# Differential attention: 1/rms of the output as a power on GpSimd in place of ScalarE's root and VectorE's reciprocal

## What is computed

```python
def rms_norm(x, g):
    x32 = x.astype(F32)
    y = x32 * lax.rsqrt(jnp.mean(x32 * x32, axis=-1, keepdims=True) + EPS)
    return (y * g.astype(F32)).astype(x.dtype)

def diff_attention_mixer(u_lat, u_ctx, w_in, w_out, qn_g, kn_g, lam_vecs, subln_g, ...):
    q, k, v, z = split(u @ w_in)            # per token, 16 heads
    q, k = rms_norm(q, qn_g), rms_norm(k, kn_g)     # over 64 features each, two halves per head
    # rotary on the latent tokens, then per head: softmax(q1 k1) - lam * softmax(q2 k2), times v
    def finish(o, z, n):
        o = rms_norm(o, subln_g) * (1.0 - lam_init)
        return (o.reshape(bsz, n, D_INNER) * jax.nn.silu(z)) @ w_out
```

## Time and profile before

| | us |
|---|---|
| median of 3 runs (lowest to highest) | 4143.25 (4135.88 to 4145.75) |
| the profiled execution's own time | 4144.13 |
| its span (first to last instruction) | 4142.5 |
| TensorE busy | 3833.1 (93%) |
| VectorE busy | 2058.4 (50%) |
| ScalarE busy | 1136.8 (27%) |
| GpSimd busy | 142.6 (3%) |

### The profile page before, as it was taken

The page is one execution under the profiler, slowest core; times in us unless marked ns, Lnnn a source line. Parts: engine busy times, 40 slices in busy tenths (PEclk is TensorE's granted clock), DMA queues, the critical chain, the costliest instruction groups (busy, mean ns, idle before and its releaser), DMA issues. The chain is left out here.

```text
span 4142.5 us, 44540 instructions
## 1 busy us (share of the span) xinstructions
PE 3833.1 (93%) x16250; PEld 2479.6 (60%) x16250; DVE 2058.4 (50%) x3726; ACT 1136.8 (27%) x2079; POOL 142.6 (3%) x227
## 2 busy tenths in 40 slices
PE   6998999998889999999999999999697999999989
PEld 2445688874445888866565656565354555555554
DVE  3743453533553635446666666666303555555540
ACT  1112100011331000103343444434100444444430
POOL 6500000000000000000000000000000000000000
PEclk8998899987998999889999999999899999999999
DMA  7521323321013332421010111111011121111111
GB/s 151 138 71 46 102 76 97 82 77 48 22 46 88 90 91 72 107 77 36 26 32 29 30 30 30 30 30 31 15 51 46 48 56 56 56 56 56 56 41 53
DMA packets 456432, 246.26 MB, mean 59 GB/s; under 512 B 44256, under 2 KB 448352, under 8 KB 456320
## 3 DMA queue, kind: packets, MB, share of 16 engines
q1 hardware_dynamic: 420384, 216.15, 18.8%
q0 software_dynamic: 14144, 28.36, 2.6%
q10 hardware_dynamic: 21792, 0.22, 0.4%
HBM read 229.83 MB, written 14.80 MB: 59 GB/s over the span
## 5 line engine op out<-in xcount | busy, mean ns | idle before, releaser
L1152 PE MATMUL bank<-hT,ring 128*128 128x512 f32 (+1 forms) x1664 | 634.0, 531 | 23.4 <-DVE hT L1527 19.8
L1628 PE MATMUL bank<-hT,ring 128*128 128x512 f32 (+1 forms) x1536 | 521.1, 491 | 21.0 <-DVE big L1880 16.3
L1152 PEld LDWEIGHTS bank<-hT,ring 128*128 128x128 f32 x1664 | 310.8, 191 | 300.8 <-issue 269.5
L1628 PEld LDWEIGHTS bank<-hT,ring 128*128 128x128 f32 x1536 | 287.4, 190 | 250.3 <-issue 212.5
L326 PE MATMUL bank<-big,ring 128*128 128x512 f32 (+1 forms) x1024 | 391.9, 546 | 12.1 <-DVE big L1892 8.4
L326 PEld LDWEIGHTS bank<-big,ring 128*128 128x128 f32 x1024 | 196.7, 192 | 206.0 <-issue 185.5
L1057 ACT ACTIVATE arena<-bank 128x512 f32<-128x512 f32 (+2 forms) x224 | 118.3, 528 | 461.7 <-PE bank L1050 461.6
L456 PE MATMUL bank<-big,arena 128*128 128x256 f32 x1024 | 228.8, 379 | 0.0
L456 PEld LDWEIGHTS bank<-big,arena 128*128 128x128 f32 x1024 | 194.6, 190 | 26.5
L1025 DVE CUSTOM_DVE_ANT_0 arena<-bank,big 128x512 f32<-128x512 f32 (+2 forms) x152 | 101.3, 666 | 199.7 <-PE bank L1005 199.7
L1623 PEld LDWEIGHTS bank<-ring,hT 128*128 128x128 f32 x1536 | 177.7, 192 | 30.4 <-DVE arena L1847 17.0
(11 more groups left out here) (278 smaller groups left out, 5515.4 us busy)
## 6 DMA issues: line engine op xcount, KB each, us to landing
ring<-in_mlp_w SPq DMA_DIRECT2D x128, 512.0 KB, 5.2
ring<-in_a_w_in SPq DMA_DIRECT2D x64, 512.0 KB, 4.0
ring<-in_b_w_in SPq DMA_DIRECT2D x64, 512.0 KB, 4.0
ring<-in_mod_w SPq DMA_DIRECT2D x48, 512.0 KB, 3.7
ring<-in_even_w_in SPq DMA_DIRECT2D x32, 512.0 KB, 4.0
bias_d<-tb POOLq DMA_DIRECT2D x96, 128.0 KB, 3.4
big<-bias_d POOLq DMA_DIRECT2D x16, 768.0 KB, 5.4
ring<-in_a_w_out SPq DMA_DIRECT2D x16, 512.0 KB, 3.7
```

The costliest lines, as they stand in the source:

```text
L1152: mm = pe.matmul(bk(b + n)[0:m, 0:z - a], ring[s][:, k, 0:m], (rhs or hcol)(k, a, z), start=k == 0, stop=k == kt - 1)
L1628: mm = pe.matmul(flatb[2][:, a:z], ring[s][:, k, :], hT[:, k, a:z], start=k == 0, stop=k == KT - 1)
```

## The change

The norm of the head's output gets its 1/rms in another way. ScalarE no longer takes a root: a new `sums` writes sum/128 + eps (Identity) from `flatb[3]` into a new tile `d_os`, a view of the first 768 columns of `tb`. GpSimd, by a new stream `pool_dif`, raises `d_os` to the power -0.5 in place (`tensor_tensor` with ALU.pow, the exponent being a column of `cols` repeated 768 times). VectorE's `y_normed` has no reciprocal any more: it waits for GpSimd's semaphore `po` and multiplies by `d_os`. The norms of q and k keep root and reciprocal in `rs`. Since the output no longer uses `rs`, some waits change. The new stream stands ahead of `pool_nat` in GpSimd's order.

```diff
+        d_os = tb[:, :, :].rearrange("p a b -> p (a b)")[:, 0:TT]
...
+            def sums(n):
+
+                act.wait_ge(ds["st"], n)
+                act.activation(d_os, flatb[3][:, 0:TT], ACT.Identity, scale=1.0 / P, bias=eps).then_inc(ds["nf"], 1)
...
             if make:
                 if old:
-                    act.wait_ge(ds["y"], h)
+                    act.wait_ge(ds["nr"], g * 2)
                 root(st.sq["q"], 64)
...
             if old:
-                if make:
-                    act.wait_ge(ds["nr"], g * 2 + 2)
-                else:
-                    act.wait_ge(ds["y"], h)
-                root(st.sq["o'"], P)
+                act.wait_ge(ds["y"], h)
+                sums(st.sq["o'"])
...
                 square(at(y2, h))
                 act.wait_ge(ds["y"], h + 1)
-                root(st.sq["o"], P)
+                sums(st.sq["o"])
...
                 dve.reciprocal(rs[:, :], rs[:, :]).then_inc(ds["rr"], 1)
-                dve.wait_ge(ds["rr"], st.sq[x])
+                dve.wait_ge(ds["rr"], g * 2 + (n + 1))
...
             def y_normed(h, x, use):
                 st.n_done(dve, use)
-                dve.reciprocal(rs[:, :], rs[:, :]).then_inc(ds["rr"], 1)
-                dve.wait_ge(ds["rr"], st.sq[x])
+                dve.wait_ge(ds["po"], h + 1)
                 dve.wait_ge(ds["y1"], h + 1)
-                dve.scalar_tensor_tensor(out=at(y2, h), in0=at(y2, h), scalar=cols[:, 9:10], in1=rs[:, :],
+                dve.scalar_tensor_tensor(out=at(y2, h), in0=at(y2, h), scalar=cols[:, 9:10], in1=d_os,
                                          op0=ALU.mult, op1=ALU.mult).then_inc(ds["y"], 1)
...
+        def pool_dif(pool, h, e, g, ge, gu, first):
+            st = Step(h, g, first)
+
+            def rooted(h, use):
+
+                st.n_done(pool, use)
+                pool.tensor_tensor(d_os, d_os, cols[:, 10:11].to_broadcast([P, TT]), ALU.pow).then_inc(ds["po"], 1)
+
+            if h is not None and not first:
+                rooted(h - 1, "so'")
+            if g is None:
+                rooted(h, "so")
...
+            pool.memset(cols[:, 10:11], -0.5)
...
         @block.gpsimd
         def _(pool):
             pool_bias(pool)
+            run_dif(pool_dif, pool)
             pool_nat(pool)
```

More of the change, by code:

```diff
@@ L1559, in program @@
                                             "sq", "st", "rr", "nr", "rot", "m1", "m2", "prod", "pv",
-                                            "y1", "y", "ax")}
+                                            "y1", "y", "ax", "po")}
         class Step:
@@ L1931, in dve_dif @@
                 y_normed(h, "o", "so")
+        def pool_dif(pool, h, e, g, ge, gu, first):
[7 more added lines that the diff above has]
+                rooted(h, "so")
         def run_dif(f, eng):
-            for x in {pe_dif: ("tp", "pv"), act_dif: ("ex",), dve_dif: ("y",)}[f]:
+            for x in {pe_dif: ("tp", "pv"), act_dif: ("ex",), dve_dif: ("y",), pool_dif: ()}[f]:
                 eng.sem_inc(ds[x], 1)
```

## The result

The changed kernel takes 6074.0 us (median of 4 runs, 6069.81 to 6076.54) against 4143.56 us before: ratio 1.4663, 95% interval 1.4637 to 1.4688. It is 1930 us slower. The direction is the one forecast, the size is not: 90 us were forecast, and the range ended at 4440.

A forecast was written before the change was run, and what follows sets the result against it. TensorE was taken to bound the full steps, a cross-engine chain the last. Terms 14 x 5.6 = 78.4, +4.6, -0.2, +6.1 and +1.3 gave +90.2 on 4144.13; forecast 4233 us (median 0.9 lower), range 4137 to 4440.

The forecast's parts named there:

- What bounds the kernel: Differential stage: TensorE bounds the full steps, busy 934 of 1000 us; the last step is a chain across engines.
- what the removals give: Output norm: removing the 4.94 us reciprocal and 1.283 us table loads gives 0 in full steps, at most 2.1 us.
- The price of the power: GpSimd: one 128 x 768 power was priced at 12 us, from its add and VectorE's reciprocal.
- D: Duration of one 128 x 768 power on GpSimd, taken as 12 us.
- The ends that it kept, 1.9 and 25.9: Bounds in us on one power: an add's price, and two reciprocal-like functions with a third for special cases.
- 16 D - 101.8: Total added time in us over 14 full steps and the last step, for D over 7.4; +90.2 as forecast.
- the likeliest one on record: Case of a lock and a power over 7.1 us: chance 0.60, range 4165 to 4440 us.
- What D meets: Full steps: the power blocks VectorE's two-input L1839 after 6.4 free us; each us beyond costs 1 us, 14 times.
- The rival without a lock: VectorE runs beside the power and waits only at `po`: chance 0.06 over 12.4 us, 0.12 up to 12.4.
- The rival's threshold of 12.1 us: Full step without a lock: time from the power's start that is free before L1892 makes `pv_out` late.
- The rival of a short power: Power below 7.1 us, mostly done before L1839: no measurable change, 4138 to 4140 us at 1.9; chance 0.19.
- The moved table load: Norm after the output projection: a 1.28 us load moves to L278, onto the path, costing +1.3 us.

The follow-up runs named there:

- Run 1: The changed kernel with GpSimd's power replaced by a product of the same operands, same waits, 1/rms left out: 4134.57 us, ratio 0.9992.
- runs 1 and 2: Run 1, and the changed kernel with the power over only 32 of 768 columns, the others keeping the mean square: the latter 4132.88 us, ratio 0.9980.
- run 5: The changed kernel with each power written as three powers of 256 columns, same work and result: 5942.86 us, ratio 1.4356.
- run 3: The kernel before plus a GpSimd power over 256 columns of an unused tile in each full step, which nobody waits for: 4146.27 us.

## Why the prediction was wrong

**What bounds the kernel, and what the removals give: right.** The reciprocal lay in TensorE's shadow. Run 1 has it away, with a cheap operation in its place, and gains nothing that can be measured.

**The price of the power: the step that failed.** The prediction took D = 12 us, between one and two functions of the reciprocal's cost. D is 122.6 us. The ends that it kept, 1.9 and 25.9, did not hold it either. The factor 5.2 between VectorE's reciprocal and its plain pass was carried over to another engine and another operation, and nothing in the trace says that GpSimd's power is built like VectorE's reciprocal: it is 84 times GpSimd's own product of 1.47 us. The upper end stood on a count of functions and was no bound. With D = 122.6 the prediction's own sum, 16 D - 101.8, gives 1860 us, 96% of the loss. So the case was the likeliest one on record, and its largest term was too small by a factor of ten.

**What D meets: the path right, the first instruction held not.** VectorE is held by a long power, in the changed kernel; but the first to be held is the negation L1824, 3.4 us after the power's start, not L1839 after 6.4. Over 14 steps that is 14 x 3.0 = 42 us. The clock's fall in the idle time, 2.1 us a step in the mean or 29 us, was left out. The two together are the 70 us that the sum is short of.

What the prediction took from the add (a two-input VectorE instruction does nothing until GpSimd has ended) is too strong even for the add: L895 ends 0.39 us after it and needs some 0.6, so it was let go 0.2 us before the end. It holds for the product of run 1 in the same way. For a power it does not hold: a two-input instruction is let go within the first us where the power has 256 or 512 columns, and after 81 to 82 us where it has 576 or 768. The page of the Trainium skill that was weighed there (SBUF — State Buffer, Who interferes with whom) counts two-port instructions in; the trace agrees in so far as a one-input instruction from SBUF to SBUF was the one held longest. Its rule that the pair is held for the whole instruction did not show here: a power of 61.5 us held none of the instructions that came during it, and one of 122.6 let a two-input instruction go after 82.6.

**The rival without a lock** had the mechanism that sets the size: once the power is cut in parts of up to 512 columns, the time is 5943 by the wait at `po` alone. The rival's threshold of 12.1 us fits: 123.3 us of power gave a mean step of 182.8, and 69.8 + (123.3 - 12.1) = 181.0. The other 1.8 us are in line with the matrix products behind the pause, of which the first 32 take 13.40 us instead of 10.59. Lock or wait, at D = 122.6 each is ruinous, and they differ by 8 us a step. The prediction held the two to be rivals; the code has both, and the later of them counts.

**The rival of a short power** is what runs 1 and 2 show: at 1.5 and 5.4 us no loss, under a lock or not.

**The moved table load** was wrong in its place: it runs in idle time ahead of its wait, and costs 0.

What stays open: why a column of a power costs 0.16 us on GpSimd, and whether that depends on the exponent. On the values it did not depend here: 256 columns take 41.1 us with mean squares (run 5) and with a tile filled with 1.5 (run 3). No run had a power on VectorE, nor one with a number for the exponent in place of a tensor. Nor is it shown what singles out the negation, which is held to the end: it and L1842, the two that were held long, both read `cols`, the tile that the exponent comes from, and L1888 and L1820, which passed, do not. Beside powers of up to 512 columns reads of `cols` were not held, so a shared tile alone does not do it; a long power with its exponent in another tile was not run.

## What to carry to other kernels

Before work is moved to an engine that has never run that operation, measure one instruction of it; a price carried over from another engine's operation can be off by a factor of ten, and its "upper end" with it. A long wait in one instruction says who was held, not what the loss is: take the hold away and see whether the time moves (here 131 us of 1930). Removing work in a shadow gives nothing; root and reciprocal replaced in all three norms, two of them (q and k) on a chain that TensorE waits for, gave 0.9%, once the bank was released at the first moment it could be.

## What the runs showed of the hardware that was not expected

- A power on GpSimd (fp32, exponent from a repeated column) takes 5.41 us for 32 columns, 41.1 for 256, 61.5 for 384, 81.9 for 512, 92.2 for 576 and 122.6 for 768: 0.159 us a column and some 0.3 fixed. It is the same for 1 partition as for 128. A product of 768 columns takes 1.47 us.
- A power of up to 512 columns held a two-input VectorE instruction only at its start, by less than 1 us, and none that came later. One of 576 or 768 columns held the two-input L1842 for 82.24 and 82.56 us, about what 512 columns take (81.9), and the small one-input negation to its own end. That GpSimd reads up to 512 columns at 1.7 ns each, works on them, reads the rest, and keeps its claim on reading until the last column is read fits all seven widths and these four times; it is an inference.
- A product of 768 columns on GpSimd (1.47 us) made a two-input VectorE instruction that began beside it 1.12 us longer.
- ScalarE's table load for a later root (L278 in run 1) began 8.05 us before that root, ahead of its wait, and cost nothing. At the last root of the stage the load came behind the wait, on the path.
